# One ring for the two halves of a weight piece, with its blocks in pairs, and 96 products without a use at the end

## The chip, the cores and the metric

The kernel runs on one core of one Trainium2 chip. The metric is the device time of one execution in microseconds; the median of three runs of the kernel before is 2080.28 us (2080.0 to 2080.88).

## The reference, cut to what matters

Two layers of a trunk for 256 tokens of 2048 channels, all in float32, then a last RMSNorm. For each layer:

```
h = rmsnorm(x);  p = h @ w_in                 # 2048 x 4608, cut into q, k, v, pooling and convolution inputs
x = x + concat(attention, convolution, pooling) @ w_out        # 2048 x 2048
gu = rmsnorm(x) @ w_ffn_in                    # 2048 x 11008
x = x + (silu(conv3(gu[:, :5504])) * gu[:, 5504:]) @ w_ffn_out # 5504 x 2048
```

Nearly all work lies in these four products by a weight matrix.

## The kernel before, in words

**The stream of weights.** All four weight matrices are cut into blocks of 128x128 and stored in the order of use, eight blocks to a piece of 128x1024 (512 KB): 728 pieces, 364 for each layer, and two of zeros behind them. SyncE's queue loads a piece into one of the four slots of the ring `raw` (`load`, L335 to L339). ScalarE copies it, rounded, into `whi` (`hi`, L391 to L406, the copy on L406), and VectorE subtracts that from the piece and writes what is left to `wlo` (`lo`, L732 to L736). `whi` and `wlo` are two rings of four slots like `raw`; block number blk of a slot begins at column 128 x blk. TensorE waits for `lo_ready`; when the last product of a piece is done, `slot_free` (or `acc_done` at the end of a group) lets ScalarE refill the slot. The first two pieces are converted ahead of the loops, the first in two halves, by `high_half` (L363) and `low_half` (L714).

**The moving side.** The activations are stored as halves too: `xg`, `mix` and `hidden` hold for each chunk k of 128 channels 256 columns of high halves and, behind them, 256 columns of low halves.

**The products.** `group` (L1194) makes four tiles of 128 output channels at once, one PSUM bank each, over nk chunks. For each block it issues a `high_product` (L1178: whi block stationary, all 512 columns moving, L1179) and a `low_product` (L1181: wlo block stationary, the 256 high columns moving, L1182). They are issued in pairs, two high products, then their two low ones:

```
for n in range(0, len(order), 2):
    pair = order[n:n + 2]
    # ... high_product for both of the pair, then low_product for both
```

In the middle pieces of a group a piece's eight blocks are taken in the order in which they lie (two chunks k, four tiles i each). In the first piece (where nothing else is awaited) and the last one, `order.sort(key=lambda o: (o[3], o[2]))` takes them tile by tile, so that a pair is block i and block i + 4. The last group pair of the feed-forward input has three tiles and not four, so that eight blocks of a piece are two chunks and two thirds there.

In two places the roles are exchanged and the activations are stationary: `v_group` (L1239, products on L1255 to L1257), which makes the values of the attention, and `token_group` (L1440, products on L1456 to L1458), which makes the last product of layer 1. There 512 columns of whi or wlo move.

**The order of the rest.** Each engine walks the same list of pieces; work beside the stream (attention, convolution, norms, evacuations) is hung on a piece's number by `at(idx, fn)` and runs behind that piece.

**Where things lie.** The tiles are placed one behind the other in the order in which they are declared, with small unused tiles (`offset0` to `offset3`) between some of them. By the declared sizes `whi` begins 51,136 bytes behind `xg` (32,768 of xg, 1,024 of ssq, 960 of offset1, 16,384 of raw), which is 64 bytes short of a multiple of 512; `hidden1`, layer 1's hidden tile, begins 55,296 bytes behind `whi`, which is 108 times 512.

**The end.** Behind the last product of `token_group(3)` VectorE adds the residual from PSUM banks 6 and 7 (`token_sums`, L970), ScalarE squares (L564), both scale (L693, L1129, L1131), and SyncE issues eight stores (L351) and waits for them.

Of the kernel before, what the change touches and what calls it, by code (L numbers as in the profile page):

```python
# [23 lines left out]
LAYERS = 2  # L24
DM = 2048
S = 256
P = 128
# [10 lines left out]
RING = 4  # L38
PB = 8
PIECE = PB * P  # L40
# [3 lines left out]
CV, CG, V0, Q0, K0, Q1, K1, V1, PO = range(9)  # L44
# [14 lines left out]
D0 = CT + 12  # L59
# [7 lines left out]
TD = TT + 2 * NT  # L67
TILES = TD + 16
CREDIT = 8
# [23 lines left out]
assert sum(TAPS_AT.values()) == (CONV_K - 1) * NT  # L93

WARM = 6
COLS = NT * P
FRONT = 3 * COLS
STORES = ((1, 0), (0, 0), (1, 1), (1, 2), (0, 1), (0, 2), (1, 3), (0, 3))
# [33 lines left out]
def program(nc, xT, wstream, params, lamv, consts, poolw, pww, gain_rows, outT):  # L132
# [4 lines left out]
    f32, f32r = mybir.dt.float32, mybir.dt.float32r  # L137
    ALU, ACT, AX = mybir.AluOpType, mybir.ActivationFunctionType, mybir.AxisListType

    ctx = ExitStack()  # L140
    with ctx:
        def sb(name, shape, dt=f32, where=ctx):
            return where.enter_context(nc.sbuf_tensor(name, shape, dt))
# [2 lines left out]
            return ctx.enter_context(nc.semaphore(name))  # L146


        x = sb("x", [P, KC, S])
        sb("offset0", [P, 16])  # L150
        with ExitStack() as until_ffn_out:
# [6 lines left out]
        ssq = sb("ssq", [P, S])  # L158
        sb("offset1", [P, 240])
        raw = sb("raw", [P, RING, PIECE])  # L160
        whi = sb("whi", [P, RING, PIECE], f32r)
        wlo = sb("wlo", [P, RING, PIECE], f32r)
        con = sb("con", [P, NCON])
        par = sb("par", [P, NPAR + 1])
        credit = sb("credit", [P, 2])
# [33 lines left out]
        hidden1 = sb("hidden1", [P, FC, 2 * S], f32r)  # L199
# [18 lines left out]
        hi_ready = sem("hi_ready")  # L218
        lo_ready = sem("lo_ready")
# [137 lines left out]
        def _(act):  # L357
# [3 lines left out]
                                     scale=par[:, gains + c:gains + c + 1]).then_inc(xhi_ready, 1)  # L361

            def high_half(s, a, b, done):  # L363
                nc.scalar.activation(whi[:, s, a:b], raw[:, s, a:b], ACT.Copy).then_inc(done, 1)  # L364

            act.dma_start(x[:, 0:2, :], xT[:, 0:2, :]).then_inc(x_loaded[0], 16)
            act.dma_start(par[:, P_NN:P_NN + KC], params[LAYERS][:, 0:KC]).then_inc(gain_loaded, 16)
# [18 lines left out]
            for l in range(LAYERS):  # L386
                hidden = hidden_of[l]
                def hi(idx, rel, count=None):

                    s = rel % RING  # L390
                    act.wait_ge(raw_landed[s], (l * (PIECES // RING) + (idx - s) // RING + 1) * 16  # L391
                                if isinstance(idx, int) else count[2])

                    if isinstance(idx, int):
                        old = idx - RING
                        if old < 0:
                            pass
                        elif old in ENDS:
                            act.wait_ge(acc_done, l * TILES + ENDS[old] + 1 + DONE0)
                        else:  # L400
                            act.wait_ge(slot_free, l * SLOT_INCS + slot_count(old) + SLOT0)
                    elif count[0] == "tile":
                        act.wait_ge(acc_done, count[1])
                    else:
                        act.wait_ge(slot_free, count[1])
                    nc.scalar.activation(whi[:, s, :], raw[:, s, :], ACT.Copy).then_inc(hi_ready, 1)  # L406

                def halves(tile, banks, scales=(1.0,) * NT):
                    for i, b in enumerate(banks):
# [287 lines left out]
        def _(dve):  # L697
# [15 lines left out]

            def low_half(s, a, b, done, count):  # L714
                dve.wait_ge(done, count)
                nc.vector.tensor_tensor(wlo[:, s, a:b], raw[:, s, a:b], whi[:, s, a:b], ALU.subtract).then_inc(lo_ready, 1)  # L716

            dve.wait_ge(gain_loaded, 16)
            gain_lo(0, P_NN, 1)
# [8 lines left out]
            for l in range(LAYERS):  # L728
# [3 lines left out]
                def lo(idx, rel):  # L732

                    s = rel % RING
                    dve.wait_ge(hi_ready, l * PIECES + idx + 1)
                    nc.vector.tensor_tensor(wlo[:, s, :], raw[:, s, :], whi[:, s, :], ALU.subtract).then_inc(lo_ready, 1)  # L736

                def add_halves(tile, banks, dst, h0, scales=None):
                    for i, b in enumerate(banks):
# [431 lines left out]
        def _(pe):  # L1171
# [4 lines left out]
            for l in range(LAYERS):  # L1176
                hidden = hidden_of[l]
                def high_product(bank, s, blk, mov, first):  # L1178
                    nc.tensor.matmul(ps[bank][:], whi[:, s, blk * P:blk * P + P], mov, start=first, stop=False)  # L1179

                def low_product(bank, s, blk, mov, last):  # L1181
                    return nc.tensor.matmul(ps[bank][:, 0:S], wlo[:, s, blk * P:blk * P + P], mov[:, 0:S],  # L1182
                                            start=False, stop=last)

                hooks = {}
# [53 lines left out]
                def v_group(piece0, tile, free, banks):  # L1239

                    for p in range(8):
                        s = (piece0 + p) % RING
                        arrived(piece0 + p)
                        order = [(kk, t) for kk in range(2) for t in range(2)]
                        if p in (0, 7):
                            order.sort(key=lambda o: o[1])
                        for n, (kk, t) in enumerate(order):
                            k, bank = 2 * p + kk, ps[banks[t]][:]
                            if k == 0:
                                pe.wait_ge(evacuated, l * TILES + free[t] + CREDIT)  # L1250
                            xh = xg[:, k, t * P:t * P + P]
                            xl = xg[:, k, S + t * P:S + t * P + P]
                            wh = whi[:, s, kk * 512:kk * 512 + 512]
                            wl = wlo[:, s, kk * 512:kk * 512 + 512]
                            nc.tensor.matmul(bank, xh, wh, start=k == 0, stop=False)  # L1255
                            nc.tensor.matmul(bank, xh, wl, start=False, stop=False)  # L1256
                            last = nc.tensor.matmul(bank, xl, wh, start=False, stop=k == KC - 1)  # L1257
                            if k == KC - 1:
                                last.then_inc(acc_done, 1)
                            elif n == 3:  # L1260
                                last.then_inc(slot_free, 1)
                        for fn, args in hooks.get(piece0 + p, ()):
                            fn(*args)
# [170 lines left out]
                def token_group(g):  # L1434
                    batches = [(p,) for p in range(DP - 2)] + [(DP - 2, DP - 1)]
                    for batch in batches:
                        order = [(p, kk, t) for p in batch for kk in range(2) if 2 * p + kk < FC for t in range(2)]
                        if batch[0] == 0 or len(batch) == 2:
                            order.sort(key=lambda o: o[2])
                        first_of = {p: min(n for n, o in enumerate(order) if o[0] == p) for p in batch}  # L1440
                        last_of = {p: max(n for n, o in enumerate(order) if o[0] == p) for p in batch}
                        for n, (p, kk, t) in enumerate(order):
                            k, s, bank = 2 * p + kk, (D0 + DP * g + p) % RING, ps[2 * g + t][:]
                            if n == first_of[p]:
                                arrived(D0 + DP * g + p)
                            if g == 0 and k % NT == 0 and t == 0:
                                pe.wait_ge(hidden_ready, l * FFG + k // NT + 1)
                            if k == 0:
                                pe.wait_ge(evacuated, l * TILES + (TT + NT if g < 2 else TD) + CREDIT)
                                if g == 3:  # L1450
                                    pe.wait_ge(x_copied, 8)
                            xh = hidden[:, k, t * P:t * P + P]
                            xl = hidden[:, k, S + t * P:S + t * P + P]
                            wh = whi[:, s, kk * COLS:kk * COLS + COLS]
                            wl = wlo[:, s, kk * COLS:kk * COLS + COLS]
                            nc.tensor.matmul(bank, xh, wh, start=k == 0, stop=False)  # L1456
                            nc.tensor.matmul(bank, xh, wl, start=False, stop=False)  # L1457
                            last = nc.tensor.matmul(bank, xl, wh, start=False, stop=k == FC - 1)  # L1458
                            if k == FC - 1:
                                last.then_inc(acc_done, 1 if t == 0 else NT - 1)  # L1460
                            elif n == last_of[p]:
                                last.then_inc(slot_free, 1)
                        for p in batch:
                            for fn, args in hooks.get(D0 + DP * g + p, ()):
                                fn(*args)
# [7 lines left out]
                with pe.Fori(0, 2) as d:  # L1473
                    for u in range(2):
                        tile = TD + 4 * u
                        group(d * (2 * DP) + D0 + DP * u, 0, [d * 8 + (tile + i + 1 - 8) for i in range(4)],
                              range(4 * u, 4 * u + 4), FC, lambda k: hidden[:, k, :],
                              (lambda k: pe.wait_ge(hidden_ready, l * FFG + k // NT + 1) if k % NT == 0 else None)
                              if u == 0 else None, rel0=D0 + DP * u, hook=False)

    assert SEEN == STEPS, (SEEN, STEPS)

# [82 lines left out]
```

## Time and profile before

| | |
|---|---|
| median of three runs | 2080.28 us |
| runs | 2080.0, 2080.88, 2080.28 us |
| span of the profiled execution, first to last instruction | 2078.2 us |
| TensorE | 2064.8 us busy, 99% |
| VectorE | 1415.6 us busy, 68% |
| ScalarE | 1081.7 us busy, 52% |
| mean granted TensorE clock | 0.998 |
| DMA | 392.66 MB, mean 189 GB/s |

The page gives the profiled execution's span and no device time of its own. The runs lie 1.8 to 2.7 us above the span: this is what lies before the first and behind the last instruction. A matmul's record reaches from its start to its modelled end, so records overlap; how fast TensorE really steps is read from one start to the next.

### The profile page before, as it was taken

The numbers are of one execution on the slowest core, as the hardware profiler recorded it, in microseconds if no ns is written. First come the engines' busy times: TensorE is split into PE (matmuls) and PEld (weight loads), VectorE is DVE, ScalarE is ACT, GpSimd is POOL, SyncE is SP. The second block draws the span as 40 slices with busy tenths as digits, with TensorE's granted clock in tenths as the row PEclk, the third lists the DMA queues.
The fourth block names the chain that finished last, engine by engine and source line by source line (L and its number), as shares of the span: only waits on it lengthen the run. The fifth ranks groups of instructions, "written<-read, shape, count | busy, mean of one in ns | idle before, by whom it ended". The sixth has DMA issues, their size and how long they took to land.

```text
span 2078.2 us, 32569 instructions
## 1 busy us (share of the span) xinstructions
PE 2064.8 (99%) x11564; PEld 1792.4 (86%) x11564; DVE 1415.6 (68%) x2009; ACT 1081.7 (52%) x1509; POOL 23.5 (1%) x20
## 2 busy tenths in 40 slices
PE   9999999999999999999999999999999999999998
PEld 8888888888888888888888888888888888888886
DVE  7998777676666666555489978676666676654454
ACT  6556655555555554433374566455555555544444
POOL 0001100000000000000000011000000000000000
PEclk9999999999999999999999999999999999999999
DMA  8554455655555555555666544655555655565664
GB/s 290 179 183 159 139 183 182 204 190 192 192 182 192 191 192 193 193 197 179 207 209 196 177 145 145 198 190 192 191 184 182 202 189 195 183 212 193 194 199 163
DMA packets 108944, 392.66 MB, mean 189 GB/s; under 512 B 12225, under 2 KB 12737, under 8 KB 108481
## 3 DMA queue, kind: packets, MB, share of 16 engines
q1 hardware_dynamic: 106992, 386.45, 56.6%
q10 hardware_dynamic: 1872, 5.13, 0.8%
q8 instruction: 54, 0.88, 0.2%
q14 instruction: 26, 0.20, 0.0%
HBM read 389.43 MB, written 2.10 MB: 188 GB/s over the span
## 4 chain that ended last, share of the span: by engine, by line
PE 99%; DMA 0%; DVE 0%; ACT 0%; ACTq 0%; issue 0%; DVEq 0%
PE bank L1179 53%; PE bank L1182 27%; PE bank L1458 4%; PE bank L1457 4%; PE bank L1456 4%; PE bank L1266 2%; PE bank L1255 1%; PE bank L1256 1%; PE bank L1257 1%; DMA x<-xT 0%; PE bank L1319 0%; PE bank L1431 0%; PE bank L1342 0%; DVE xt L1131 0%; DVE wlo L716 0%; ACT whi L364 0%
## 5 line engine op out<-in xcount | busy, mean ns | idle before, releaser
L736 DVE TENSOR_TENSOR wlo<-raw,whi 128x1024 fp32r<-128x1024 f32 x728 | 885.8, 1222 | 609.5 <-ACT whi L406 608.6
L1179 PE MATMUL bank<-xg,whi 128*128 128x512 f32 x3648 | 1135.6, 393 | 1.9 <-DVE wlo L716 1.9
L406 ACT ACTIVATE whi<-raw 128x1024 fp32r<-128x1024 f32 x728 | 764.2, 1057 | 693.3 <-PE bank L1182 558.0
L1182 PEld LDWEIGHTS bank<-xg,wlo 128*128 128x128 f32 x3648 | 685.0, 188 | 151.3
L1182 PE MATMUL bank<-xg,wlo 128*128 128x256 f32 x3648 | 720.1, 279 | 0.0
L1179 PEld LDWEIGHTS bank<-xg,whi 128*128 128x128 f32 x3648 | 552.9, 188 | 6.3 <-issue 3.3
L1179 PE MATMUL bank<-hidden,whi 128*128 128x512 f32 x688 | 213.5, 392 | 0.0
L1179 PE MATMUL bank<-mix,whi 128*128 128x512 f32 x512 | 160.7, 395 | 0.0
L1182 PEld LDWEIGHTS bank<-hidden,wlo 128*128 128x128 f32 x688 | 129.2, 188 | 28.5
L1182 PE MATMUL bank<-hidden,wlo 128*128 128x256 f32 x688 | 135.8, 279 | 0.0
L1456 PE MATMUL bank<-whi,hidden 128*128 128x512 f32 x344 | 134.6, 391 | 0.0
L1458 PE MATMUL bank<-whi,hidden 128*128 128x512 f32 x344 | 134.0, 389 | 0.0
L1457 PE MATMUL bank<-wlo,hidden 128*128 128x512 f32 x344 | 133.9, 389 | 0.0
L411 ACT ACTIVATE half<-bank 128x256 f32<-128x256 f32 x228 | 86.1, 382 | 62.4 <-PE bank L1182 59.9
L1182 PEld LDWEIGHTS bank<-mix,wlo 128*128 128x128 f32 x512 | 96.1, 188 | 21.2
L1179 PEld LDWEIGHTS bank<-hidden,whi 128*128 128x128 f32 x688 | 104.2, 188 | 0.0
L1182 PE MATMUL bank<-mix,wlo 128*128 128x256 f32 x512 | 101.1, 279 | 0.0
L793 DVE SCALAR_TENSOR_TENSOR gt<-glu,par,gt 128x256 f32<-128x256 f32 x240 | 100.7, 477 | 0.0
L1179 PEld LDWEIGHTS bank<-mix,whi 128*128 128x128 f32 x512 | 78.3, 188 | 0.8
L1458 PEld LDWEIGHTS bank<-whi,hidden 128*128 128x128 f32 x344 | 64.6, 188 | 13.5
L1457 PEld LDWEIGHTS bank<-wlo,hidden 128*128 128x128 f32 x344 | 64.6, 188 | 13.2
L1456 PEld LDWEIGHTS bank<-whi,hidden 128*128 128x128 f32 x344 | 64.6, 188 | 13.2
(150 smaller groups left out, 1140.8 us busy)
## 6 DMA issues: line engine op xcount, KB each, us to landing
raw<-wstream SPq DMA_DIRECT2D x729, 512.0 KB, 3.4
pw_sb<-pww ACTq DMA_DIRECT2D x2, 1024.0 KB, 7.3
outT<-xt SPq DMA_DIRECT2D x8, 256.0 KB, 2.9
x<-xT SPq DMA_DIRECT2D x2, 512.0 KB, 10.3
gains<-gain_rows ACTq DMA_DIRECT2D x1, 1024.0 KB, 6.3
raw<-wstream SPq DMA_DIRECT2D x2, 256.0 KB, 4.5
x<-xT ACTq DMA_DIRECT2D x2, 256.0 KB, 5.4
x<-xT SPq DMA_DIRECT2D x2, 256.0 KB, 7.3
```

The lines of the kernel that those rows point to most:

```text
L406: nc.scalar.activation(whi[:, s, :], raw[:, s, :], ACT.Copy).then_inc(hi_ready, 1)
L411: nc.scalar.activation(half[:, i, :], ps[b][:, S:2 * S], ACT.Copy, scale=scales[i]).then_inc(half_ready, 1)
L736: nc.vector.tensor_tensor(wlo[:, s, :], raw[:, s, :], whi[:, s, :], ALU.subtract).then_inc(lo_ready, 1)
L793: ins = nc.vector.scalar_tensor_tensor(out=gt[:, i, 0:S], in0=glu[:, i, k:k + S], scalar=w, in1=gt[:, i, 0:S], op0=ALU.mult, op1=ALU.add)
L1179: nc.tensor.matmul(ps[bank][:], whi[:, s, blk * P:blk * P + P], mov, start=first, stop=False)
L1182: return nc.tensor.matmul(ps[bank][:, 0:S], wlo[:, s, blk * P:blk * P + P], mov[:, 0:S], start=False, stop=last)
L1255: nc.tensor.matmul(bank, xh, wh, start=k == 0, stop=False)
L1256: nc.tensor.matmul(bank, xh, wl, start=False, stop=False)
L1266: return nc.tensor.matmul(out, lhsT, rhs, start=first, stop=last)
L1456: nc.tensor.matmul(bank, xh, wh, start=k == 0, stop=False)
L1457: nc.tensor.matmul(bank, xh, wl, start=False, stop=False)
L1458: last = nc.tensor.matmul(bank, xl, wh, start=False, stop=k == FC - 1)
```

## The change

The two rings `whi` and `wlo` become one ring `halves_of` of twice the width, in the same place. For most pieces a slot is cut into four stretches of 512 columns, each of which holds two low blocks and then the two high blocks that belong to them. For the pieces of `v_group` and of `token_group` (`straight`) a slot holds all high columns and then all low ones, since 512 columns in a row are read as the moving side there. The conversions on ScalarE and VectorE write and read accordingly. Behind the last group of layer 1 TensorE issues 96 products whose results nobody reads, from `hidden1` into banks 0 to 3: four lists of places (PROBES), six pairs for each, two high and two low products to a pair.

```diff
+PROBES = (((0, 0), (2, 1), (1, 2), (3, 3)), ((0, 2), (2, 3), (3, 1), (1, 0)), ((0, 3), (2, 2), (1, 1), (3, 0)),
+          ((0, 2), (2, 3), (1, 1), (3, 0)))
...
+        def straight(l, rel):
+            return rel // PB in (V0, V1) or (l == LAYERS - 1 and rel >= D0)
+
+        def parts(s, a=0, b=PIECE, whole=False):
+
+            if whole:
+                return raw[:, s, a:b], halves_of[:, s, a:b], halves_of[:, s, PIECE + a:PIECE + b]
+            pairs = halves_of[:, s, 2 * a:2 * b].rearrange("p (q h c) -> p q h c", h=2, c=2 * P)
+            return raw[:, s, a:b].rearrange("p (q c) -> p q c", c=2 * P), pairs[:, :, 1, :], pairs[:, :, 0, :]
...
-        whi = sb("whi", [P, RING, PIECE], f32r)
-        wlo = sb("wlo", [P, RING, PIECE], f32r)
+        halves_of = sb("halves_of", [P, RING, 2 * PIECE], f32r)
...
-                nc.scalar.activation(whi[:, s, a:b], raw[:, s, a:b], ACT.Copy).then_inc(done, 1)
+                source, high, _ = parts(s, a, b)
+                nc.scalar.activation(high, source, ACT.Copy).then_inc(done, 1)
...
-                    nc.scalar.activation(whi[:, s, :], raw[:, s, :], ACT.Copy).then_inc(hi_ready, 1)
+                    source, high, _ = parts(s, whole=straight(l, rel))
+                    nc.scalar.activation(high, source, ACT.Copy).then_inc(hi_ready, 1)
...
-                nc.vector.tensor_tensor(wlo[:, s, a:b], raw[:, s, a:b], whi[:, s, a:b], ALU.subtract).then_inc(lo_ready, 1)
+                source, high, low = parts(s, a, b)
+                nc.vector.tensor_tensor(low, source, high, ALU.subtract).then_inc(lo_ready, 1)
...
-                    nc.vector.tensor_tensor(wlo[:, s, :], raw[:, s, :], whi[:, s, :], ALU.subtract).then_inc(lo_ready, 1)
+                    source, high, low = parts(s, whole=straight(l, rel))
+                    nc.vector.tensor_tensor(low, source, high, ALU.subtract).then_inc(lo_ready, 1)
...
-                    nc.tensor.matmul(ps[bank][:], whi[:, s, blk * P:blk * P + P], mov, start=first, stop=False)
+                    _, high, _ = parts(s)
+                    nc.tensor.matmul(ps[bank][:], high[:, blk // 2, blk % 2 * P:blk % 2 * P + P], mov, start=first, stop=False)
...
-                    return nc.tensor.matmul(ps[bank][:, 0:S], wlo[:, s, blk * P:blk * P + P], mov[:, 0:S],
+                    _, _, low = parts(s)
+                    return nc.tensor.matmul(ps[bank][:, 0:S], low[:, blk // 2, blk % 2 * P:blk % 2 * P + P], mov[:, 0:S],
                                             start=False, stop=last)
...
-                            wh = whi[:, s, kk * 512:kk * 512 + 512]
-                            wl = wlo[:, s, kk * 512:kk * 512 + 512]
+                            _, wh, wl = parts(s, kk * COLS, kk * COLS + COLS, whole=True)
...
-                            wh = whi[:, s, kk * COLS:kk * COLS + COLS]
-                            wl = wlo[:, s, kk * COLS:kk * COLS + COLS]
+                            _, wh, wl = parts(s, kk * COLS, kk * COLS + COLS, whole=True)
...
+            flat = hidden1[:].rearrange("p k c -> p (k c)")
+            moving, weights = flat[:, 16:16 + 2 * S], flat[:, 4 * S:]
+            pe.wait_ge(evacuated, (LAYERS - 1) * TILES + TD + 8 + CREDIT)
+            for places in PROBES:
+                for pair in range(6):
+                    for n, (w, q) in enumerate(places):
+                        b, o = 2 * (pair % 2) + w // 2, weights[:, q * P:q * P + P]
+                        if w % 2 == 0:
+                            nc.tensor.matmul(ps[b][:], o, moving, start=True, stop=False)
+                        else:
+                            nc.tensor.matmul(ps[b][:, 0:S], o, moving[:, 0:S], start=False, stop=True)
```

## Rows read from the trace of the kernel before

**Rows 1.** The page's busy times, and the first two lines of its chain.

```profile
PE 2064.8 (99%) x11564; PEld 1792.4 (86%) x11564; DVE 1415.6 (68%) x2009; ACT 1081.7 (52%) x1509; POOL 23.5 (1%) x20
...
PE 99%; DMA 0%; DVE 0%; ACT 0%; ACTq 0%; issue 0%; DVEq 0%
PE bank L1179 53%; PE bank L1182 27%; PE bank L1458 4%; PE bank L1457 4%; PE bank L1456 4%; PE bank L1266 2%; PE bank L1255 1%; PE bank L1256 1%; PE bank L1257 1%; DMA x<-xT 0%; PE bank L1319 0%; PE bank L1431 0%; PE bank L1342 0%; DVE xt L
```

**Rows 2.** Waits of TensorE: us in total, times, longest us.

```profile
PE bank L1179 <- DVE wlo L716: 1.9, 2, 1.6
```

**Rows 3.** Page, part 5, products by form: count, busy us, mean ns.

```profile
L1179 PE MATMUL bank<-xg,whi 128*128 128x512 f32 x3648 | 1135.6, 393 | 1.9 <-DVE wlo L716 1.9
...
L1182 PE MATMUL bank<-xg,wlo 128*128 128x256 f32 x3648 | 720.1, 279 | 0.0
...
L1179 PE MATMUL bank<-hidden,whi 128*128 128x512 f32 x688 | 213.5, 392 | 0.0
L1179 PE MATMUL bank<-mix,whi 128*128 128x512 f32 x512 | 160.7, 395 | 0.0
...
L1182 PE MATMUL bank<-hidden,wlo 128*128 128x256 f32 x688 | 135.8, 279 | 0.0
...
L1182 PE MATMUL bank<-mix,wlo 128*128 128x256 f32 x512 | 101.1, 279 | 0.0
```

**Rows 4.** Chain in pieces taken tile by tile: start us, us, what.

```profile
411.74 0.46 PE bank L1179 x2
412.20 0.23 PE bank L1182 x2
412.42 0.46 PE bank L1179 x2
...
414.50 0.46 PE bank L1179 x2
```

**Rows 5.** The same in the groups of three tiles.

```profile
769.84 0.46 PE bank L1179 x2
770.30 0.24 PE bank L1182 x2
...
771.22 0.46 PE bank L1179 x2
```

**Rows 6.** Windows: six pieces in order, three-tile groups: us, PE busy (count).

```profile
417.10:433.66 16.56, 16.56 (x99) 14.57 (x98) 10.25 (x9) 7.34 (x7) 0.00 (x0) 1.00 0.59 194
767.70:800.73 33.03, 33.03 (x193) 29.06 (x192) 23.37 (x30) 17.57 (x22) 0.00 (x0) 1.00 0.58 190
```

**Rows 7.** Timeline of TensorE in the first group of values: start us, us.

```profile
175.84 0.39 PE L1256 MATMUL bank<-wlo,xg 128*128 128x512 f32 x1
...
178.17 0.40 PE L1257 MATMUL bank<-whi,xg 128*128 128x512 f32 x1
```

**Rows 8.** The same behind the last wait, in the last group of tokens.

```profile
2064.98 0.39 PE L1458 MATMUL bank<-whi,hidden 128*128 128x512 f32 x1
...
2067.70 0.39 PE L1458 MATMUL bank<-whi,hidden 128*128 128x512 f32 x1
```

**Rows 9.** Page, part 5, the two conversions.

```profile
L736 DVE TENSOR_TENSOR wlo<-raw,whi 128x1024 fp32r<-128x1024 f32 x728 | 885.8, 1222 | 609.5 <-ACT whi L406 608.6
...
L406 ACT ACTIVATE whi<-raw 128x1024 fp32r<-128x1024 f32 x728 | 764.2, 1057 | 693.3 <-PE bank L1182 558.0
```

**Rows 10.** Groups of VectorE by form: rows with a step, and without.

```profile
L981 DVE TENSOR_TENSOR gt<-gt,rstd 128x1024 f32<-128x1024 f32 x20 | 24.5, 1226 | 0.7
...
L1006 DVE TENSOR_TENSOR half<-half,y 128x1024 f32<-128x1024 f32 x20 | 24.4, 1218 | 0.0
```

**Rows 11.** Windows: VectorE's fullest stretch, and the end (PE, PEld, DVE, ACT, POOL).

```profile
104.00:156.00 52.00, 52.00 (x316) 44.86 (x314) 49.53 (x112) 29.04 (x57) 0.00 (x0) 1.00 0.55 183
2064.00:2078.00 14.00, 4.09 (x19) 3.04 (x17) 5.45 (x10) 6.23 (x11) 0.00 (x0) 0.74 0.40 150
```

**Rows 12.** Timeline of the end, all engines.

```profile
2068.20 0.69 DVE L970 TENSOR_TENSOR xt<-bank,xt 128x512 f32<-128x512 f32 x1 [1.17 <-PE bank L1458]
...
2070.92 4.46 SPq L351 DMA_DIRECT2D outT<-xt  x8
```

**Rows 13.** Page, part 6, the stores: us from issue to landing.

```profile
outT<-xt SPq DMA_DIRECT2D x8, 256.0 KB, 2.9
```

## The prediction, made before the changed kernel was built or run

> **What bounds the kernel now.** I read the page's busy times and its chain first [rows 1]: TensorE is busy 99% of 2078.2 us, and the chain that ended last runs through it for 99%, half of it through the high products (L1179) and a quarter through the low ones (L1182). Then I asked what TensorE waited for [rows 2]: 1.9 us for converted weights in two waits of the start, and nothing on the conversion of the 728 later pieces. So ScalarE, VectorE and the stream of DMAs are hidden, and two things can move the time: the step from one product to the next, and work before or behind the stream.
>
> The mean of a record says nothing about the step, since records overlap: its 393 and 279 ns [rows 3] are longer than the steps. The step is the distance between starts. In pieces taken tile by tile a pair begins at 411.74, the next at 412.42, and the fifth at 414.50 [rows 4]: 2.76 us for four pairs, so two high and two low products take 0.69 us. At 2.4 GHz, the level granted nearly all the time (mean 0.998), their 1536 columns last 0.64 us, so 50 ns in a set of four products, 12.5 ns in each, are not columns. There are 3648 + 688 + 512 = 4848 high products and as many low ones [rows 3], that is 2424 sets of four: 1673 us at 0.69, and 121 us of them are this extra. That is what a placement could touch.
>
> **Does the extra depend on where the blocks lie?** The trace has the experiment in it, because the order of the blocks varies. I number the four block places of a 2 KB stretch 0 to 3. In order, a set reads high 0, 1 and low 0, 1, the next high 2, 3 and low 2, 3. Tile by tile a set reads place 0 four times, then place 1 four times, and so on. In the groups of three tiles the places walk on against the chunks from piece to piece. Tile by tile a set takes 0.69 [rows 4]. In the three-tile groups 769.84 to 771.22 is 1.38 for two sets [rows 5], and their whole stretch of 192 products takes 33.03, that is 172 ns for each. Six pieces in order, 96 products, take 16.56, that is 172.5 ns each [rows 6]; the counts there take in products that overlap the edges. All three are 0.69 for four. Next loads in places 0, 1, 2 and 3, behind high and behind low products, cost the same. The new ring reads high 2, high 3, low 0, low 1: each of these four has stood behind such a product already.
>
> What a placement does change is seen where the roles are exchanged. In a group of values a step of 512 columns takes 233 ns: 175.84 to 178.17 is 2.33 for ten steps [rows 7]. In the last group of tokens it is 227 ns: 2064.98 to 2067.70 is 2.72 for twelve [rows 8]. The same columns and the same form of product, 6.6 ns apart. By the declared sizes the stationary block begins 64 bytes further within 512 than the moving one in the values, and level with it in the tokens; in the main groups it is 64 bytes less. So the offset within 512 bytes may matter. The change moves every block by a multiple of 512 bytes from the same base, and keeps these offsets in all three kinds of product. **Cost of the new placement on TensorE: 0.** Bounds: one such observed difference of 6.6 ns on each of 9696 products, 64 us, in either direction. I take 0, because rows 4 to 6 are of the very products that change and show no difference.
>
> By the Trainium skill (TensorE: Matmul & The Clock Gate, Back-to-back issue gap) a warm product that stands alone in its step takes N/2.4 + 2.5 ns, so four would take 650 ns and not the 690 that the trace shows. The trace decides for the sum; by the page 40 ns of each set would be there to be won, 97 us in all, if the extra were a matter of layout.
>
> **The conversions.** Their number stays, no DMA and no wait is moved, and no queue is passed. What is new is that ScalarE writes four stretches of 256 columns with a step, and VectorE reads and writes such stretches. Now they take 1057 and 1222 ns [rows 9]. The nearest rows: a VectorE operation of the same size on rows with a step took 1226 ns, one without 1218 [rows 10]. So 8 ns for each operation, 5.8 us of VectorE's time over 728 pieces, all beside TensorE; nothing to 8 ns is the bound from rows. The cover is thinnest at 104 to 156 us, where VectorE is busy 49.53 of 52 us [rows 11]: some 19 pieces pass there, so it holds until an operation costs 130 ns more. Uncovered are only the conversions ahead of the first product, two small ones on each engine: at most 0.03 us. **Cost: 0.**
>
> **The added products.** 96 products behind the last group, 4 lists x 6 pairs x 4. Their wait is for the evacuation of the groups of banks 0 to 3, which is two groups old by then (2 x 258 products at 0.227, some 117 us); behind it on TensorE stand only these products, and nobody waits for them. They write banks 0 to 3, while VectorE reads 6 and 7, so the tail is not held up. TensorE has been busy at full clock until then. Their moving side begins 64 bytes behind a multiple of 512 from the stationary one, which is the offset of the main groups. So each set takes 0.69 and all of them 24 x 0.69 = 16.56 us, exactly as the six pieces in rows 6.
>
> They begin one step behind the last real product, at 2067.70 + 0.23 = 2067.93 [rows 8], and the last of them, a low one, starts at 2067.93 + 16.56 - 0.12 = 2084.37 and ends 0.28 later, at **2084.65**. Beside this the old tail runs as it did: the sum at 2068.20, the eight stores issued from 2070.92 to 2075.38 [rows 12], the last landing 2.9 us later [rows 13] at about 2078.3, the old end. So 10.1 of the 16.6 us are hidden by the tail, and TensorE becomes the one that ends last, 6.4 us later than the old end. A restart behind the wait may add 0.1.
>
> **Sum.** 2078.2 + 6.4 = 2084.6 for the span. The runs lie 2.1 above the profiled span in the median, the page having no device time of its own, so 2080.3 + 6.4 = **2086.7 us**, 0.31% slower. I take 0.2% (4.2 us) as what a measurement of this kernel can tell from no change.
>
> **The rivals.**
> *The new placement makes the step shorter.* For it: 12.5 ns in each product are no columns, and 6.6 ns did depend on layout once [rows 7, 8]. Against it: three different walks over the places all took 0.69 [rows 4 to 6]. At 6.6 ns a product the time is 2086.7 - 64 = 2023. From 0.24 ns a product on it would fall within 0.2% of before, from 1.1 ns on it would be faster by more. Chance 6%; I give it no more, since no row of these products shows even 0.24.
> *The new placement makes it longer*, by the same rows: 2086.7 + 64 = 2151. Chance 5%.
> *The added products do not count.* If the time ended with the last store, or if they went twice as fast, everything would lie in the tail's shadow, and the time would be 2080.3. For it: 10 of the 16.6 us are hidden anyway, and 6.4 are not far from 4.2. Against it: the span goes to the last instruction of any engine, and the products cannot go below 24 x 0.64 = 15.4 us, which still ends at 2083.5. Chance 5%.
> *The conversions lose their cover.* It begins at 130 ns an operation in one stretch, sixteen times the row's 8 ns; at 200 ns the 19 pieces there and as many in layer 1 would cost 2 x 19 x 0.07 = 2.7 us, 2089.4. Chance 2%.
>
> **How the numbers follow.** The forecast has 82%; its own range is 2085.5 to 2088, from the restart, the steps of the four lists and the distance of span and runs. The range 2083.5 to 2089 takes in also a shorter step of the added products, and some of the conversions' case; the two large cases of placement and the shadow, 16% together, lie outside. Faster: 6%. Same: the shadow and small gains, 6%. Slower: 88%.
>
> **What would show it.** In the changed kernel's profile: 0.69 for a set of four in the same three stretches, and the first start of the first added product near 2067.9; conversions of 1057 to 1065 and 1222 to 1230 ns; no new wait of TensorE; granted clock 1.0 to about 2084 where it was 0.74 on average behind 2064 [rows 11]; TensorE alone in the last 6 us. Wrong I would be by any other figure than 0.69, for the main groups first: 1 ns in a product is 9.7 us.

## The result and the profile after

The changed kernel takes 2087.09 us in the median (2086.8 to 2087.46, 6 runs) against 2080.2 us (2080.0 to 2081.12, 6 runs): 6.9 us longer, ratio 1.0033 with a 95% interval of 1.0021 to 1.0044. The forecast was 2086.7. The profiled execution's span is 2085.2 us where it was 2078.2. Run by run the time lies some 1.9 us above that run's own span (1.85 to 1.95 in nearly all of them), so the 1.8 to 2.7 given for the kernel before came from setting three runs against the span of a single one. One of the ten executions of the kernel with half the added products took 2563.38 us at a mean granted clock of 0.752 and is left out below.

The page's first line of busy times and its chain, against [rows 1]:

```profile
PE 2081.3 (100%) x11660; PEld 1807.7 (87%) x11660; DVE 1415.9 (68%) x2009; ACT 1081.7 (52%) x1509; POOL 23.5 (1%) x20
...
PE bank L1195 53%; PE bank L1199 27%; PE bank L1473 4%; PE bank L1471 4%; PE bank L1472 4%; PE bank L1282 2%; PE bank L1271 1%; PE bank L1272 1%; PE bank L1273 1%; PE bank L1504 1%; DMA x<-xT 0%; PE bank L1506 0%; PE bank L1335 0%; PE bank 
```

L1195 and L1199 are the old L1179 and L1182. The shares are the old ones; new are 1% for L1504, the added high products, and L1506, the low ones, which rounds to 0%. TensorE's busy time grew by 16.5 us and the span by 7.0.

The chain in pieces that are taken tile by tile, start and us (to be read as [rows 4]):

```profile
412.02 0.46 PE bank L1195 x2
412.48 0.23 PE bank L1199 x2
412.70 0.46 PE bank L1195 x2
...
414.78 0.46 PE bank L1195 x2
```

412.02 to 414.78 is 2.76 for four sets of two high and two low products, 0.69 each. In order, with the new places 2, 3, 0, 1:

```profile
418.23 0.45 PE bank L1195 x2
...
418.92 0.46 PE bank L1195 x2
...
420.99 0.46 PE bank L1195 x2
```

That is again 2.76 for four. In the groups of three tiles, as in [rows 5]:

```profile
770.12 0.46 PE bank L1195 x2
...
771.50 0.46 PE bank L1195 x2
```

1.38 for two sets. The windows of [rows 6] and [rows 11] (us, then busy time and count of PE, PEld, DVE, ACT, POOL, then granted clock, DMA share, GB/s):

```profile
417.10:433.66 16.56, 16.56 (x97) 14.58 (x96) 10.50 (x9) 7.34 (x7) 0.00 (x0) 1.00 0.56 193
767.70:800.73 33.03, 33.03 (x193) 29.12 (x192) 23.55 (x29) 17.42 (x23) 0.00 (x0) 1.00 0.59 193
104.00:156.00 52.00, 52.00 (x315) 44.99 (x314) 49.55 (x112) 29.06 (x57) 0.00 (x0) 1.00 0.56 183
2064.00:2085.00 21.00, 20.96 (x116) 18.00 (x114) 5.45 (x10) 6.25 (x11) 0.00 (x0) 1.00 0.27 101
```

The same 16.56 and 33.03 us hold the same number of products but for records that cross an edge, VectorE's fullest stretch went from 49.53 to 49.55 us, and TensorE's clock stays at 1.00 to the end. The waits of TensorE and the conversions, against [rows 2] and [rows 9]:

```profile
PE bank L1195 <- DVE halves_of L730: 2.3, 2, 1.2
```

```profile
L751 DVE TENSOR_TENSOR halves_of<-raw,halves_of 128x1024 fp32r<-128x1024 f32 x728 | 886.5, 1223 | 609.4 <-ACT halves_of L419 608.7
...
L419 ACT ACTIVATE halves_of<-raw 128x1024 fp32r<-128x1024 f32 x728 | 764.3, 1057 | 692.4 <-PE bank L1199 561.0
```

2.3 us of waits in the start where it was 1.9, and 1223 and 1057 ns for a conversion where it was 1222 and 1057. Writing in stretches with a step costs at most 1 ns. Last the end, from the timeline of all engines:

```profile
2067.98 0.39 PE L1473 MATMUL bank<-halves_of,hidden 128*128 128x512 f32 x1
...
2068.20 0.63 PE L1504 MATMUL bank<-hidden 128*128 128x512 f32 x2
...
2068.47 0.69 DVE L985 TENSOR_TENSOR xt<-bank,xt 128x512 f32<-128x512 f32 x1 [1.17 <-PE bank L1473]
...
2071.19 4.47 SPq L362 DMA_DIRECT2D outT<-xt  x8
...
2084.56 0.40 PE L1506 MATMUL bank<-hidden 128*128 128x256 f32 x2
```

The last real product starts at 2067.98 and the first added one 0.22 later, without a pause for its wait. VectorE's sum (2068.47) and the stores (2071.19) follow as before, 0.27 later than in [rows 12] since the whole stream ran that much later in this execution. The last pair of low products starts at 2084.56.

### The profile page after: what moved, and what is told of

It reads as the page before. It is cut to its first block, busy times and chain, and to the rows that moved or that the text cites. A ratio compares the mean times of both kernels' runs of the same rounds, so it can differ in the third digit from the quotient of the medians.

```text
span 2085.2 us, 32761 instructions
## 1 busy us (share of the span) xinstructions
PE 2081.3 (100%) x11660; PEld 1807.7 (87%) x11660; DVE 1415.9 (68%) x2009; ACT 1081.7 (52%) x1509; POOL 23.5 (1%) x20
## 4 chain that ended last, share of the span: by engine, by line
PE 99%; DMA 0%; ACT 0%; DVE 0%; ACTq 0%; issue 0%
PE bank L1195 53%; PE bank L1199 27%; PE bank L1473 4%; PE bank L1471 4%; PE bank L1472 4%; PE bank L1282 2%; PE bank L1271 1%; PE bank L1272 1%; PE bank L1273 1%; PE bank L1504 1%; DMA x<-xT 0%; PE bank L1506 0%; PE bank L1335 0%; PE bank L1447 0%; PE bank L1358 0%; DVE halves_of L730 0%
## 5 line engine op out<-in xcount | busy, mean ns | idle before, releaser
L751 DVE TENSOR_TENSOR halves_of<-raw,halves_of 128x1024 fp32r<-128x1024 f32 x728 | 886.5, 1223 | 609.4 <-ACT halves_of L419 608.7
L1195 PE MATMUL bank<-xg,halves_of 128*128 128x512 f32 x3648 | 1135.8, 393 | 2.3 <-DVE halves_of L730 2.3
L419 ACT ACTIVATE halves_of<-raw 128x1024 fp32r<-128x1024 f32 x728 | 764.3, 1057 | 692.4 <-PE bank L1199 561.0
L1199 PEld LDWEIGHTS bank<-xg,halves_of 128*128 128x128 f32 x3648 | 685.1, 188 | 151.0
L1199 PE MATMUL bank<-xg,halves_of 128*128 128x256 f32 x3648 | 721.1, 279 | 0.0
L1195 PEld LDWEIGHTS bank<-xg,halves_of 128*128 128x128 f32 x3648 | 553.0, 188 | 6.7 <-issue 3.3
L1195 PE MATMUL bank<-hidden,halves_of 128*128 128x512 f32 x688 | 213.4, 392 | 0.0
L1195 PE MATMUL bank<-mix,halves_of 128*128 128x512 f32 x512 | 160.8, 395 | 0.0
L1199 PEld LDWEIGHTS bank<-hidden,halves_of 128*128 128x128 f32 x688 | 129.2, 188 | 28.4
L1199 PE MATMUL bank<-hidden,halves_of 128*128 128x256 f32 x688 | 136.0, 279 | 0.0
L1471 PE MATMUL bank<-halves_of,hidden 128*128 128x512 f32 x344 | 134.7, 392 | 0.0
L1473 PE MATMUL bank<-halves_of,hidden 128*128 128x512 f32 x344 | 134.1, 390 | 0.0
L1472 PE MATMUL bank<-halves_of,hidden 128*128 128x512 f32 x344 | 134.0, 389 | 0.0
L1199 PEld LDWEIGHTS bank<-mix,halves_of 128*128 128x128 f32 x512 | 96.2, 188 | 21.1
L1195 PEld LDWEIGHTS bank<-hidden,halves_of 128*128 128x128 f32 x688 | 104.3, 188 | 0.0
L1199 PE MATMUL bank<-mix,halves_of 128*128 128x256 f32 x512 | 101.2, 279 | 0.0
L1195 PEld LDWEIGHTS bank<-mix,halves_of 128*128 128x128 f32 x512 | 78.3, 188 | 0.8
L1473 PEld LDWEIGHTS bank<-halves_of,hidden 128*128 128x128 f32 x344 | 64.6, 188 | 13.5
L1472 PEld LDWEIGHTS bank<-halves_of,hidden 128*128 128x128 f32 x344 | 64.6, 188 | 13.2
L1471 PEld LDWEIGHTS bank<-halves_of,hidden 128*128 128x128 f32 x344 | 64.6, 188 | 13.0
```

What stands on the lines that cost most here:

```text
L419: nc.scalar.activation(high, source, ACT.Copy).then_inc(hi_ready, 1)
L751: nc.vector.tensor_tensor(low, source, high, ALU.subtract).then_inc(lo_ready, 1)
L1195: nc.tensor.matmul(ps[bank][:], high[:, blk // 2, blk % 2 * P:blk % 2 * P + P], mov, start=first, stop=False)
L1199: return nc.tensor.matmul(ps[bank][:, 0:S], low[:, blk // 2, blk % 2 * P:blk % 2 * P + P], mov[:, 0:S], start=False, stop=last)
```

## The experiments

Medians in us; each ratio is to runs of the kernel before on the same chip.

| run | median | kernel before | ratio, 95% interval |
|---|---|---|---|
| e1_layout_alone | 2080.1 | 2080.09 | 1.0000 (0.9991 to 1.0009) |
| e2_products_alone | 2086.95 | 2080.09 | 1.0032 (1.0020 to 1.0044) |
| e3_half_products | 2080.66 | 2080.09 | 1.0002 (0.9992 to 1.0011) |
| e4_double_products | 2103.4 | 2080.09 | 1.0112 (1.0097 to 1.0128) |
| e5_offsets | 2187.62 | 2080.61 | one run each |
| e6_two_offsets | 2363.17 | 2080.21 | one run each |
| e7_ring_shifted | 2099.63 | 2080.27 | 1.0092 (1.0077 to 1.0108) |
| e8_values_shifted | 2078.4 | 2080.27 | 0.9990 (0.9981 to 0.9999) |

### The layout alone

```diff
-            flat = hidden1[:].rearrange("p k c -> p (k c)")
-            moving, weights = flat[:, 16:16 + 2 * S], flat[:, 4 * S:]
-            pe.wait_ge(evacuated, (LAYERS - 1) * TILES + TD + 8 + CREDIT)
-            for places in PROBES:
...
```

> The changed kernel without the 96 added products: the one ring and its placements stay. My theory (the placement costs nothing, the added products cost all): 2080.3 us, within 0.7 of the kernel before; a set of two high and two low products takes 0.69 us; the span ends with the last store at about 2078.3. Rival (the new placement is slower, the added products are hidden in the tail): 2086 to 2087. Rival (the new placement is faster by some ns a product and hides part of the added products' cost): below 2078.

Measured 2080.1 against 2080.09 us. The new ring costs nothing that can be measured, and the stretch in order is the old one:

```profile
417.10:433.66 16.56, 16.56 (x97) 14.59 (x97) 10.49 (x10) 7.34 (x7) 0.00 (x0) 1.00 0.57 190
```

Its profiled span is 2079.2 and not 2078.2. Laid start by start beside the kernel before, that 1.0 us is complete by 12 us and changes by at most 0.07 us from there to the last product, so over 2056 us of products the two placements step alike. The 1.0 us is the clock at the start, as the windows show, this kernel first and then the kernel before:

```profile
8.47:11.88 3.41, 3.41 (x13) 2.92 (x12) 3.03 (x5) 3.19 (x6) 0.00 (x0) 0.50 1.03 415
8.47:11.88 3.41, 3.11 (x18) 2.52 (x18) 2.90 (x5) 3.06 (x6) 0.00 (x0) 1.00 1.03 416
```

In this execution the granted clock was 0.50 (1.2 GHz) over these 3.4 us, in the other 1.00 (2.4 GHz); just before, TensorE had waited 1.96 us for its first weights here and 1.64 there. The same fall stands in the profiled execution of the kernel before with the added products, so it does not come from the new ring. The spans of the executions without a trace, of this kernel and of the one before, fall into two groups, 2077.9 to 2078.4 and 2078.7 to 2079.2; that the upper one is this fall of the clock is likely and not shown. The chain in that stretch shows one thing more:

```profile
9.23 0.85 PE bank L1195 x2
...
10.51 0.85 PE bank L1195 x2
```

At 1.2 GHz a set of two high and two low products takes 1.28 us, which is its 1536 columns and nothing else. The 50 ns of a set that are no columns are there at 2.4 GHz alone.

### The added products alone

Against the kernel before:

```diff
+            flat = hidden1[:].rearrange("p k c -> p (k c)")
+            moving, weights = flat[:, 16:16 + 2 * S], flat[:, 4 * S:]
+            pe.wait_ge(evacuated, (LAYERS - 1) * TILES + TD + 8 + CREDIT)
+            for places in PROBES:
...
```

> The kernel before, two rings as they were, with the 96 added products behind its last group. My theory: 2086.9 to 2087.1 us, the same as the changed kernel. Rival (the placement costs something): as much under 2087.1 as the layout alone lies above the kernel before.

Measured 2086.95, the changed kernel 2087.09. So the two parts add up, 0.0 and 6.9, and the whole difference is that of the added products. The two rivals about the placement are out in both directions: the interval of the layout alone leaves 1.9 us to either side, which is 0.2 ns in each of the 9696 products.

### Half and twice the added products

```diff
-            for places in PROBES:
+            for places in PROBES[0:2]:
```

> The changed kernel with the first two of the four lists, 48 products. They take 8.3 us from about 2068.2, so they end near 2076.5, before the last store lands. My theory (only what reaches past the tail counts): 2080.3 us. Rival (each added product counts in full, e.g. because something waits for TensorE's end): 2080.3 + 3.4 = 2083.7.

```diff
-            for places in PROBES:
+            for places in PROBES + PROBES:
```

> The changed kernel with the four lists issued twice, 192 products. My theory: the second 96 have no cover, 2087.1 + 16.6 = 2103.7 us, and each set takes 0.69 as the first ones do. Rival (the 6.9 us that the change cost are a fixed cost of letting TensorE end last): less than 16.6 more.

Half of them: 2080.66, within the interval no change, where a full price for each would have given 2083.7. TensorE's last pair there, from its timeline:

```profile
2075.90 0.40 PE L1506 MATMUL bank<-hidden 128*128 128x256 f32 x2
```

It ends by 2076.3 while the span ends at 2078.1 with the last store. Twice as many: 2103.4, that is 16.3 us more than the changed kernel, for 16.56 forecast:

```profile
2100.68 0.40 PE L1506 MATMUL bank<-hidden 128*128 128x256 f32 x2
```

By the trace, the 192 products take from 2067.77 to 2100.80, first start to last, 33.04 us for 191 steps or 0.69 for a set. So the cost is the time by which TensorE outlasts the last store: nothing for 48 products, 6.9 us for 96, and for each one more 172 ns by the trace and 170 by the medians. Some 9.7 us of the added products are hidden in both, 16.6 - 6.9 and 33.1 - 23.3.

### What offset costs

```diff
+OFFSETS = (0, 4, 8, 16, 24, 32, 48, 64, 80, 96, 112, 120)
...
+            for at_ in OFFSETS:
+                moving = flat[:, at_:at_ + 2 * S]
+                for pair in range(6):
...
+            for at_ in OFFSETS:
+                moving = flat[:, at_:at_ + 2 * S]
+                for n in range(24):
+                    nc.tensor.matmul(ps[n % 4][:], weights[:, n % 4 * P:n % 4 * P + P], moving, start=True, stop=True)
```

> The changed kernel with other added products: twelve offsets of the moving side against the stationary blocks within 512 bytes (0, 4, 8, 16, 24, 32, 48, 64, 80, 96, 112 and 120 floats of 4 bytes), 24 products each in sets of two high and two low ones, then 24 each with 512 columns throughout. My theory (the offset within 512 bytes sets the 12.5 ns in each product that are no columns, the block place does not): at 16 floats a set takes 0.69; at 0 floats a 512-column product takes 227 ns as in the token groups; at 112 floats it takes 233 ns as in the value groups; the other offsets lie between 213 and 250 ns and differ from one another by several ns. Rival (offset has no part, the value groups are slower for another reason, e.g. the tile that is stationary): all offsets the same to 1 ns.

Time of eight products from start to start behind the first eight of each 24, in ns, and below it that of eight products of 512 columns each:

```
floats          0     4     8    16    24    32    48    64    80    96   112   120
high, low    1394  1393  1387  1380  1400  1394  1387  1393  1392  1393  1387  1400
512 columns  1824  1853  1867  1831  1862  1866  1866  1814  1835  1868  1866  1867
```

The offset counts, and 256 bytes (64 floats) further the second row's values return within 10 ns: 0 and 64, 16 and 80, 32 and 96, 48 and 112. (In the first row 80 floats stand at 1392, and at 1380 in the next eight.) No offset takes away the part that is no columns, as the theory would have had it. In the chain's pieces the step of a set at 16 floats (2082.50 and on) and at 24 (2086.66 and on):

```profile
2082.50 0.46 PE bank L1506 x2
...
2084.57 0.46 PE bank L1506 x2
...
2086.66 0.47 PE bank L1506 x2
...
2088.76 0.47 PE bank L1506 x2
```

2.07 for three sets, then 2.10. Two windows hold 24 steps of 512 columns each, at 64 and at 112 floats:

```profile
2157.55:2163.01 5.46, 5.46 (x25) 4.51 (x24) 0.00 (x0) 0.00 (x0) 0.00 (x0) 1.00 0.00 0
2174.11:2179.72 5.61, 5.61 (x26) 4.49 (x25) 0.00 (x0) 0.00 (x0) 0.00 (x0) 1.00 0.00 0
```

5.46 and 5.61 us for 24: 227 and 234 ns. These are the token groups' and the value groups' steps ([rows 8] and [rows 7]), whose offsets are 0 and 48 within 64 floats. So the 6.6 ns between them, which were the bound of the forecast, are the offset. For mixed sets, as in the main groups, these twelve offsets differ by less: from the best to the worst it is 20 ns in eight products, 2.5 ns in each.

### Two offsets apart, and other shapes

```diff
+            for high in range(0, 64, 8):
+                for low in range(0, 64, 8):
+                    for pair in range(6):
+                        b = 2 * (pair % 2)
+                        for w, at_, c in (("H", 2 * P + 64 - high, 0), ("H", 3 * P + 64 - high, 1),
+                                          ("L", 64 - low, 0), ("L", P + 64 - low, 1)):
+                            one(w, at_, b + c)
+            for kinds, places, banks in SHAPES:
...
```

> The changed kernel with other added products: sets of two high and two low ones, the offset of the moving side against the high blocks and against the low blocks set apart, each 0 to 56 floats in steps of 8, 24 products for each of the 64 couples; then at 16 floats six shapes of 24 products: as they are, high and low in turn, four high and four low, one bank alone, one block place alone, low ones alone. My theory (what counts is where the next stationary block is read against the running moving side, so the two kinds have optima of their own): the couples 16/16, 24/24 and 0/0 repeat 0.69, 0.70 and 0.697 for a set, and some couple of two unlike offsets takes less than 0.69. Rival (there is one best offset for both and 12.5 ns are a fixed cost of a product): no couple under 0.69, and all shapes have 12 to 14 ns for each product that are no columns, whatever bank or place.

Time of eight products, from the start of the ninth to that of the seventeenth of each 24, in ns:

```
high\low      0     8    16    24    32    40    48    56
0          1393  1394  1380  1405  1400  1400  1400  1414
8          1387  1396  1400  1400  1394  1400  1414  1400
16         1413  1427  1391  1414  1404  1400  1406  1400
24         1406  1403  1400  1400  1436  1400  1412  1400
32         1414  1400  1400  1400  1394  1400  1413  1427
40         1400  1391  1415  1400  1400  1407  1400  1400
48         1427  1388  1384  1426  1398  1400  1387  1400
56         1411  1406  1400  1406  1407  1402  1406  1412
```

The diagonal, where both kinds have the same offset, repeats e5 within 11 ns (1393, 1396, 1391, 1400, 1394 and 1387 for 0, 8, 16, 24, 32 and 48), although here the moving side stays and the blocks are moved: what counts is the distance of the two and not the place of either. A value can change from one eight to the next: the couple 24/32 stands at 1436 here and at 1398 in the next eight, while 48/0 stands at 1427 in both. No couple falls under 1380 (the couple 16/16 is at 1380 in the next eight), so the rival holds: the kernel before already has the best that this scan knows, and setting the two kinds apart gains nothing. Of the six shapes, eight products take 1380 as they are, 1380 in one bank alone, 1380 from one block place alone, 1393 with high and low in turn and 1395 with four and four; 256 columns alone take 113.4 ns a product, 6.7 more than their columns at 2.4 GHz. So at this offset bank and block place have no part in it, which is what rows 4 to 6 had said. The second half of the rival is not borne out as it stood: the part that is no columns is not 12 to 14 ns for every product but 6.7 for one of 256 columns and 13.3 or more for one of 512. Two high and two low products, each kind in a stream of its own at its best, would come to 680 ns and not 690, so 10 ns of a set lie in mixing them. What the rest consists of stays open.

### The ring shifted against xg

```diff
-        sb("offset1", [P, 240])
+        sb("offset1", [P, 232])
```

> The layout alone (no added products) with the unused tile offset1 8 floats smaller, so that the ring lies 24 and not 16 floats off xg within 64 floats; mix and hidden move along with the ring and keep their distance. The offsets run gave 1400 ns for eight products at 24 floats and 1380 at 16. My theory (the offset is what a placement can change): the 7296 products from xg are 912 groups of eight, so 2080.1 + 912 x 0.020 = 2098.3 us, with some 2 us for the value groups, whose offset was not measured; the sets of mix and hidden stay at 0.69. Rival (the added products measured something that does not carry over to the loop with its waits and conversions): under 2090.

Measured 2099.63, 19.4 us above the kernel before, for 18.2 and up to 2 forecast. A stretch of the products from xg and one of those from hidden, in the chain's pieces:

```profile
418.53 0.47 PE bank L1195 x2
...
419.23 0.47 PE bank L1195 x2
...
420.63 0.47 PE bank L1195 x2
```

```profile
950.63 0.46 PE bank L1195 x2
...
951.32 0.46 PE bank L1195 x2
...
952.70 0.46 PE bank L1195 x2
```

2.10 for three sets from xg, 2.07 for three from hidden, whose offset did not change. The value groups, for which up to 2 us had been set aside, brought 0.2 by the starts. What goes beyond the 18.2 lies in the products from xg: eight of them take 1400 ns in the feed-forward groups and mostly 1413 in the groups of the first product of a layer. Why these two differ at the same offset stays open. Thirty-two bytes of an unused tile cost nearly three times what the change under study did.

### The value groups level

```diff
-        halves_of = sb("halves_of", [P, RING, 2 * PIECE], f32r)
+        halves_of = sb("halves_of", [P, RING, 2 * PIECE + 64], f32r)
...
-                return raw[:, s, a:b], halves_of[:, s, a:b], halves_of[:, s, PIECE + a:PIECE + b]
+                return raw[:, s, a:b], halves_of[:, s, by + a:by + b], halves_of[:, s, by + PIECE + a:by + PIECE + b]
```

Here `by` is 16 for the pieces of `v_group` and 0 otherwise.

> The layout alone (no added products) with the halves of the value groups' pieces 16 floats further within their slots, each slot 64 floats longer. The moving side is then level with the stationary one within 64 floats in the value groups, as in the token groups; all other offsets stay. My theory: a 512-column product there takes 227 ns and not 233, 384 of them, 2.5 us: 2077.6 us. Rival (the value groups are slower for another reason): 2080.1. Rival (the offset counts within 512 bytes and not within 256, so that slots of 8448 bytes spoil every second slot of the main groups): above 2080.1 by some us.

Measured 2078.4 us against 2080.27, ratio 0.9990 (0.9981 to 0.9999): the only kernel here that is faster than the one before, by 1.9 us for 2.5 forecast, and the interval nearly reaches 1. The trace shows it more surely than the time. Twelve products of the value groups in a row take 2720 ns from start to start where they took 2800; ten steps of the first group, against [rows 7]:

```profile
60.11 0.39 PE L1274 MATMUL bank<-halves_of,xg 128*128 128x512 f32 x1
...
62.38 0.39 PE L1275 MATMUL bank<-halves_of,xg 128*128 128x512 f32 x1
```

That is 2.27 for ten. Laid start by start beside the kernel before, the value groups bring 1.0 us in each layer. Slots of 8448 bytes, which are an odd multiple of 256, leave eight products of the main groups at 1380, so the rival of 512 bytes is out and the period of 256 bytes holds in the kernel too.

## Why the prediction was right

**Nothing but TensorE's step and the end can move the time:** confirmed. TensorE waited 2.3 us for converted weights, all in the start; the conversions took 1223 and 1057 ns where 8 ns more were the bound, so VectorE's cover was not touched. Not thought of was the clock at the start, which moves an execution by up to 1.0 us with the old placement and with the new one.

**The new placement costs 0:** confirmed by 0.69 for a set in all three stretches and by 2080.1 us of the layout alone. The reasoning behind it, that the order of the blocks had tried the places already, is confirmed by the shape with one block place alone (1380). The offset within 512 bytes was named as what may matter; e5 and e7 show that it does, with a period of 256 bytes. The bound taken from it, 6.6 ns for each product, was right for products of 512 columns; for mixed sets one common offset makes up to 2.5, and the worst couple that repeats (1427) 5.9.

**Against the rule** that the prediction took from the Trainium skill (TensorE: Matmul & The Clock Gate, Back-to-back issue gap), 650 ns for four products, 40 ns of each set seemed there to be won. In the 64 couples of offsets, the shapes and the whole kernels no layout has a steady step under 690 ns for two high and two low products at 2.4 GHz. The traces do not agree with the rule for such products; that page of the Trainium skill itself calls it the gap of a single product in isolation.

**The added products cost 16.56 us, of which 10.1 are hidden:** measured 16.48 from the first start to the last (2068.20 to 2084.68) for 16.44 forecast; the first list took 4174 ns and the next two 4140 each, so the restart, allowed up to 0.1, is at most 0.03. The hidden part was sized a little too large: it is 9.7 us, as half and twice the products show.

**The sum:** 6.9 us for 6.4. The median of the products alone gives the same. The profiled span is 0.5 us above the 2084.65 of the forecast: 0.27 of a later stream, 0.03 of the first list and 0.24 between the end of the last product (2084.96) and the last instruction (2085.20). The 0.27 is no cost, since the stores came later by as much. The error lies in the ends that were compared: the forecast took TensorE's last end without the 0.24 behind it, but for the tail an old end of 2078.3, while the trace of the kernel before has the last store landed by 2077.75 and closes 0.46 later. With both ends taken alike, the forecast's own working would have given some 6.7.

**The rival that the products do not count** was the nearest, and only by their number: 48 of them cost nothing.

## What to carry to other kernels

Before a layout of operands is changed, look whether the trace has tried it already: loops that walk over the same data in two orders are an experiment, and equal steps in both settle it. Read the step from start to start, since the length of a record hides it. Work on TensorE behind the last real product was free here until it outlasted the last store, and from there on it cost its full length; and where TensorE bounds the kernel, the distance of moving and stationary tiles within 256 bytes is worth a scan by added products at the end of the kernel, which shows all offsets in one execution and carries over to the main groups (20 ns in eight products forecast 18 of the 19.4 us of e7).

## What was not expected of the hardware

The step of a product depends on where the moving side lies against the stationary block that is loaded meanwhile, with a period of 256 bytes: 1380 to 1427 ns for eight mixed products (1436 once), 1814 to 1868 for eight of 512 columns. The best offset is not the same for both kinds, 16 floats for the mixed sets and 0 for those of 512 columns, and exchanging the roles of two tiles turns 16 floats into 48 within 64; so the main groups (best at 16) and the value groups (best at 0) cannot both be best without a shift of one. By the Trainium skill (TensorE: Matmul & The Clock Gate, Step-by-step) the load of the next weights does not steal read bandwidth from the running product; the measured dependence on the offset speaks against taking this to mean that their places are free. Which memory or port they share there no run here shows.
